# A transformer layer on one core: token norm, input projection and channel work made one stage that goes by blocks of 512 tokens

## Chip, cores and metric

The kernel runs on one core of a Trainium2 chip. The metric is the device time of one execution in microseconds, as the median of several. A profiled execution gives the rows below.

## What is computed

One layer of a diffusion backbone: 2048 latent tokens and a prefix of 256 context tokens, width 1024. The part that matters here is the way into the token mixer (in short form):

```python
h  = rmsnorm(x) * gain * (1 + scale) + shift      # scale, shift: c @ w_mod, other values for the context
z  = h @ w_in                                     # all columns of both branches and of the merge gates
p  = z[..., columns of the state branch]          # k, v, decay, rate; of latent tokens r and gate too
p  = p + mu[0] * (prev - p) + mu[1] * (nxt - p)   # neighbours in the sequence, zeros past its ends
kk = (k * k_k) / norm_of_head(k * k_k)            # then k * k_a, r * r_k, tanh(decay), sigmoid(gate) @ g2
```

After that come two branches (retention and a state recurrence by chunks), a merge, an output projection, and 16 experts. They are the same in both kernels.

## The kernel before

The program is a list of stages (`STAGES`, L2956). Each opens a room (buffers and semaphores) and gives every engine its own instruction stream; engines meet through semaphores alone, and a room ends when all have finished. SP issues loads and stores, POOL issues some transfers too, ACT (ScalarE) and DVE (VectorE) do elementwise work, PE (TensorE) the products. The first two stages, and the stage behind them, are in question:

- `projection` first makes the modulation vectors in a room `mod` from half of `w_mod` (8 loads of 1 MB). In `norm_rows` (L2161) the 18 token tiles of 128 tokens are loaded, squared and summed (ACT, L2212), scaled and turned by PE through a diagonal matrix (L2249), modulated (ACT and DVE), and split into a high and a low part, `hT`, kept for all 2304 tokens (L2300, L2302). The other 16 loads of `w_mod` and their products (L2157) lie in the same room. In `project` (L2307) a loop goes over the 46 column tiles of 128 columns; each tile's weights are loaded once (512 KB), split into high and low by ACT (L2360) and DVE (L2381), and multiplied with every block of tokens: 5 blocks (256 + 4 x 512) for tiles 0 to 17, which the context needs as well, and 4 for the rest. A product of one column tile with one block is 24 matmuls (8 slices of the inner dimension, each high*high, high*low and low*high, L106 to L108). ACT takes the result out (L2369) and SP writes whole rows of `zT` to DRAM.
- `rwkv_channels` (L207) reads 14 of those rows back, one row of 128 channels by 2305 positions at a time, and does the shift (L293, L295), the key norms (a contraction with ones on PE, a root on ACT, L300 and a product on DVE) and the gate's contraction (L361); POOL issues the stores (L379).
- `rwkv_chunks` follows and begins with SP's load of `ident` at L487.

What sets the order is the code of each engine, as written: an engine never passes an instruction that waits.

Of the kernel before, what the change touches and what calls it, by code (L numbers as in the profile page):

```python
# [112 lines left out]
def projection(nc, T):  # L113
# [3 lines left out]
    LATE = 4 * D // 256  # L117
    with Room(nc, "prj") as room:
# [6 lines left out]
        cond = room.sb("cond", [P, KT, 32])  # L125

        with Room(nc, "mod") as r0:
            small = r0.sb("small", [P, P])
            w = [r0.sb(f"w{g}", [P, KT, 256]) for g in range(EARLY)]
# [5 lines left out]
            w_in = [r0.sem(f"w_in{g}") for g in range(EARLY)]  # L135
# [3 lines left out]
            @block.sync  # L139
            def _(sp):  # L140
                sp.dma_start(ident[:, :], T["ident"]).then_inc(const_in, 16)
                sp.dma_start(pick[:, :], T["pick2"]).then_inc(const_in, 16)
                sp.wait_ge(zeroed, 1 + START)
                sp.dma_start(small[0:8, :], T["c"].rearrange("a (t p) -> (a t) p", p=P)).then_inc(rows_in, 16)
                sp.dma_start(small[8:16, :], T["c_ctx"].rearrange("(t p) -> t p", p=P)).then_inc(rows_in, 16)
                sp.dma_start(small[32:40, :], T["norm_g"][0, 0:1, :].rearrange("a (t p) -> (a t) p", p=P)).then_inc(rows_in, 16)
                sp.dma_start(small[64:112, :], T["b_mod"].rearrange("a (t p) -> (a t) p", p=P)).then_inc(rows_in, 16)
                for g in range(EARLY):
                    sp.dma_start(w[g][:, :, :], T["w_mod"][g]).then_inc(w_in[g], 16)
# [7 lines left out]
            def _(pe):  # L157
# [10 lines left out]
                for g in range(EARLY):  # L168
                    pe.wait_ge(w_in[g], 16 + START)
                    if g >= 4:  # L170
                        pe.wait_ge(moved, g - 3 + START)
                    contract(pe, acc[g % 4], cond, w[g]).then_inc(made, 1)
# [28 lines left out]
        with Room(nc, "prh") as rh:  # L201
            hT = [rh.sb("hT_hi", [P, KT, TOK], F32R), rh.sb("hT_lo", [P, KT, TOK], F32R)]
            norm_rows(nc, T, ident, pick, rowmod, scale, biasT, cond, hT)
            project(nc, T, hT)


def rwkv_channels(nc, T):  # L207


    W = TOK + 1  # L210
    SEGS = [(0, CTX, 0), (CTX + 1, W, CTX)]
    with Room(nc, "rch", start=0) as room:
        sb, sem = room.sb, room.sem
        ones = sb("ones", [P, P])
        g2 = sb("g2", [P, HALF])
        mu = sb("mu", [P, 14, 2])
        keep = sb("keep", [P, 14])
        par = sb("par", [P, 3, 4])
        tiny = sb("tiny", [P, 1])
        X = [sb(f"X{u}", [P, W + 2]) for u in range(3)]  # L220
        Y = [sb(f"Y{u}", [P, W]) for u in range(2)]
        norm = sb("norm", [P, W])
        ks = sb("ks", [P, W])
        kkn = sb("kkn", [P, W])
        kka = sb("kka", [P, W])
        rrk = sb("rrk", [P, W])
        gate = [sb(f"gate{u}", [P, TOK]) for u in range(2)]
        acc = room.ps("acc", [P, 5, 512])
        const_in, zeroed, keep_ok = sem("const_in"), sem("zeroed"), sem("keep_ok")
        x_in = [sem(f"x_in{u}") for u in range(3)]  # L230
        scaled, half, shifted = sem("scaled"), sem("half"), sem("shifted")
        squared, summed, rooted, ks_ok, kka_ok, recip, kkn_ok = [sem(n) for n in (
            "squared", "summed", "rooted", "ks_ok", "kka_ok", "recip", "kkn_ok")]
        rrk_ok, tanh_ok, sig_ok, g_made, g_ok = [sem(n) for n in ("rrk_ok", "tanh_ok", "sig_ok", "g_made", "g_ok")]
        y_out = [sem(f"y_out{u}") for u in range(2)]
        kkn_out, kka_out, rrk_out = sem("kkn_out"), sem("kka_out"), sem("rrk_out")
        g_out = [sem(f"g_out{u}") for u in range(2)]
        BL = [(512 * b, min(512, W - 512 * b)) for b in range(5)]
        zT = T["zT"].rearrange("(n p) t -> n p t", p=P)
        tiled = {n: T[n].rearrange("(n p) t -> n p t", p=P) for n in ("kS", "kkn", "kka", "vS", "rS", "rrk", "gT")}  # L240

        JOBS = [("wa", 0, Z_WA, 8), ("gd", 0, Z_GD, 13)]
        for p in range(4):
            JOBS += [("k", p, Z_K + p, p), ("r", p, Z_R + p, 9 + p), ("v", p, Z_V + p, 4 + p)]
        xbuf = [2 if kind == "r" else None for kind, *_ in JOBS]
        for n, j in enumerate(j for j, x in enumerate(xbuf) if x is None):
            xbuf[j] = n % 2

        def earlier(j, same):

            return max((i for i in range(j) if same[i] == same[j]), default=None)

        def loaded(j):

            return sum(16 if JOBS[i][0] == "r" else 32 for i in range(j + 1) if xbuf[i] == xbuf[j])

        def y_stored(j):

            return sum({"gd": 0}.get(JOBS[i][0], 32) for i in range(j % 2, j + 1, 2))
        block = room.block()  # L260

        @block.sync
        def _(sp):
            sp.dma_start(ones[:, :], T["head_ones"]).then_inc(const_in, 16)
            sp.dma_start(g2[:, :], T["rwkv_g2"][0]).then_inc(const_in, 16)
            with nc.allow_non_contiguous_dma("channel parameters over partitions"):
                for r in range(2):
                    sp.dma_start(mu[:, :, r], T["rwkv_mu"][0, r:r + 1, :].rearrange("a (t p) -> p (a t)", p=P)).then_inc(const_in, 16)
                for j, n in enumerate(("rwkv_k_k", "rwkv_k_a", "rwkv_r_k")):
                    sp.dma_start(par[:, j, :], T[n].rearrange("a (t p) -> p (a t)", p=P)).then_inc(const_in, 16)  # L270
            sp.wait_ge(zeroed, 3)
            for j, (kind, p, row, _) in enumerate(JOBS):
                before = earlier(j, xbuf)
                if before is not None:
                    sp.wait_ge(shifted, before + 1)
                x = X[xbuf[j]]
                for lo, hi, d in SEGS[kind == "r":]:
                    sp.dma_start(x[:, 1 + lo:1 + hi], zT[row, :, d:d + hi - lo]).then_inc(x_in[xbuf[j]], 16)

        @block.vector  # L280
        def _(ve):
            for x in X:
                ve.memset(x[:, :], 0.0).then_inc(zeroed, 1)
            ve.memset(tiny[:, :], 1e-12).then_inc(zeroed, 1)
            ve.wait_ge(const_in, 16 * 7)
            ve.tensor_tensor(keep[:, :], mu[:, :, 0], mu[:, :, 1], ALU.add).then_inc(zeroed, 1)
            ve.wait_ge(zeroed, 5)
            ve.tensor_scalar(keep[:, :], keep[:, :], -1.0, 1.0, ALU.mult, ALU.add).then_inc(keep_ok, 1)
            nk = 0
            for j, (kind, p, row, m) in enumerate(JOBS):  # L290
                x, y = X[xbuf[j]], Y[j % 2]
                ve.wait_ge(scaled, j + 1)
                ve.scalar_tensor_tensor(y[:, :], x[:, 0:W], mu[:, m, 0:1], y[:, :], ALU.mult, ALU.add).then_inc(half, 1)  # L293
                ve.wait_ge(half, j + 1)
                ve.scalar_tensor_tensor(y[:, :], x[:, 2:2 + W], mu[:, m, 1:2], y[:, :], ALU.mult, ALU.add).then_inc(shifted, 1)  # L295
                if j and JOBS[j - 1][0] == "k":

                    nk += 1
                    ve.wait_ge(rooted, nk)
                    ve.reciprocal(norm[:, :], norm[:, :]).then_inc(recip, 1)  # L300
                    ve.wait_ge(recip, nk)
                    ve.wait_ge(ks_ok, nk)
                    if nk > 1:
                        ve.wait_ge(kkn_out, 32 * (nk - 1))
                    ve.scalar_tensor_tensor(kkn[:, :], ks[:, :], -1.0, norm[:, :], ALU.mult, ALU.mult).then_inc(kkn_ok, 1)

        @block.scalar
        def _(act):
            act.wait_ge(const_in, 16 * 7)
            act.wait_ge(keep_ok, 1)  # L310
            nk = nr = 0
            for j, (kind, p, row, m) in enumerate(JOBS):
                x, y = X[xbuf[j]], Y[j % 2]
                act.wait_ge(x_in[xbuf[j]], loaded(j))
                if j >= 2:
                    act.wait_ge(y_out[j % 2], y_stored(j - 2))
                    if JOBS[j - 2][0] == "gd":
                        act.wait_ge(g_made, 16)
                act.activation(y[:, :], x[:, 1:1 + W], ACT.Copy, scale=keep[:, m:m + 1]).then_inc(scaled, 1)
                if j and JOBS[j - 1][0] == "k":  # L320

                    act.wait_ge(summed, nk)
# [1838 lines left out]
def norm_rows(nc, T, ident, pick, rowmod, scale, biasT, cond, hT):  # L2161
# [4 lines left out]
    with Room(nc, "nrm") as r1:  # L2166
# [39 lines left out]
        def _(act):  # L2206
# [11 lines left out]
            for n in range(NT):  # L2218
                u, r = n % 2, int(n < CT)
                if n + 1 < NT:  # L2220
                    sums_of(n + 1)
# [759 lines left out]
```

## Time and profile before

| | |
|---|---|
| median of three runs | 4955.49 us (4953.42 to 4962.13) |
| profiled execution, time | 4957.77 us |
| its span in the profile | 4956.0 us |
| TensorE busy | 4224.6 us (85%) |
| VectorE / ScalarE / GpSimd busy | 2297.6 / 1958.7 / 503.1 us |
| mean granted TensorE clock | 0.929 |
| moved by DMA | 637.78 MB, mean 129 GB/s |

The 1.8 us between time and span lie outside the profile. The three stages named above take the first 1438.43 us of the span.

### The profile page before, as it was taken

To read this page: it belongs to the slowest core of one execution; us is meant where nothing else is said; L and a number is where in the kernel's file an instruction comes from. 1 tells how busy PE (TensorE), PEld (TensorE's weight loads), DVE (VectorE), ACT (ScalarE), POOL (GpSimd) and SP (SyncE) were. 2 spreads that over 40 slices of the span, in tenths; PEclk is the share of its full clock that TensorE was granted. 3 is DMA by queue.
4 is the path that set the end of the run, shared out by engine and by line. 5 is a ranking of instruction groups with operands and counts; after the bars stand their busy time and mean duration, and the time that the engine had idled before them with its cause. 6 is when DMAs were issued, how large, how long until landed. Compare 5 with 4: busy or idle time off the path is not lost. (4 is left out here: it accounts for less than half of the span.)

```text
span 4956.0 us, 77358 instructions
## 1 busy us (share of the span) xinstructions
PE 4224.6 (85%) x29616; PEld 3561.7 (72%) x29616; DVE 2297.6 (46%) x3350; ACT 1958.7 (40%) x2956; POOL 503.1 (10%) x463
## 2 busy tenths in 40 slices
PE   6899999996229999999999968598946999999992
PEld 5788888885018888888888857476835888888882
DVE  4000000001656666666666658543564444444444
ACT  5111111112425655556555623511313444444443
POOL 0000000000121111111111103321001000000000
PEclk8999999998659999999999989599968999999996
DMA  7111121223641111211112133765416666666667
GB/s 281 68 69 69 68 76 64 76 76 106 244 159 47 46 46 50 58 46 46 46 48 59 46 111 103 195 228 184 161 50 246 214 220 208 207 216 216 216 207 271
DMA packets 348335, 637.78 MB, mean 129 GB/s; under 512 B 41772, under 2 KB 271636, under 8 KB 317896
## 3 DMA queue, kind: packets, MB, share of 16 engines
q1 hardware_dynamic: 328744, 542.95, 32.5%
q0 software_dynamic: 19488, 93.46, 5.8%
q8 instruction: 63, 1.03, 0.1%
q14 instruction: 40, 0.33, 0.0%
HBM read 474.92 MB, written 161.42 MB: 128 GB/s over the span
## 5 line engine op out<-in xcount | busy, mean ns | idle before, releaser
L106 PE MATMUL zp__acc<-prh__hT_hi,zp__wh 128*128 128x512 f32 (+1 forms) x1616 | 614.7, 380 | 9.4 <-DVE zp__wl L2381 9.4
L107 PE MATMUL zp__acc<-prh__hT_hi,zp__wl 128*128 128x512 f32 (+1 forms) x1616 | 614.6, 380 | 0.0
L108 PE MATMUL zp__acc<-prh__hT_lo,zp__wh 128*128 128x512 f32 (+1 forms) x1616 | 614.3, 380 | 0.0
L2040 DVE TENSOR_TENSOR exp__wl<-exp__raw,exp__wh 128x4096 fp32r<-128x4096 f32 x97 | 429.1, 4424 | 330.7 <-ACT exp__wh L1992 330.7
L2381 DVE TENSOR_TENSOR zp__wl<-zp__w,zp__wh 128x1024 fp32r<-128x1024 f32 x48 | 58.9, 1226 | 1009.5 <-ACT zp__wh L2360 1009.5
L1992 ACT ACTIVATE exp__wh<-exp__raw 128x4096 fp32r<-128x4096 f32 x97 | 352.2, 3631 | 291.3 <-PE exp__acc L108 191.6
L2369 ACT ACTIVATE zp__zo<-zp__acc 128x512 f32<-128x512 f32 (+1 forms) x202 | 117.0, 579 | 883.8 <-PE zp__acc L108 883.8
L106 PE MATMUL exp__acc<-exp__wh,exp__xh 128*128 128x512 f32 x1024 | 401.5, 392 | 2.5 <-DVE exp__xl L2045 2.5
L107 PE MATMUL exp__acc<-exp__wh,exp__xl 128*128 128x512 f32 x1024 | 399.2, 390 | 0.0
L108 PE MATMUL exp__acc<-exp__wl,exp__xh 128*128 128x512 f32 x1024 | 399.1, 390 | 0.0
L106 PEld LDWEIGHTS zp__acc<-prh__hT_hi,zp__wh 128*128 128x128 f32 x1616 | 305.1, 189 | 67.1 <-DVE zp__wl L2381 9.7
L107 PEld LDWEIGHTS zp__acc<-prh__hT_hi,zp__wl 128*128 128x128 f32 x1616 | 305.1, 189 | 57.4
L108 PEld LDWEIGHTS zp__acc<-prh__hT_lo,zp__wh 128*128 128x128 f32 x1616 | 305.0, 189 | 57.5
L599 ACT ACTIVATE rwc__Tb<-rwc__TP 128x512 bf16<-128x512 f32 x432 | 234.6, 597 | 279.5 <-PE rwc__TP L950 279.5
L799 DVE TENSOR_TENSOR rwc__Xb<-rwc__XB,rwc__level 128x512 bf16<-128x512 f32 x432 | 277.1, 683 | 110.5 <-PE rwc__XB L941 110.5
L106 PEld LDWEIGHTS exp__acc<-exp__wh,exp__xh 128*128 128x128 f32 x1024 | 192.7, 188 | 44.2 <-issue 2.9
L108 PEld LDWEIGHTS exp__acc<-exp__wl,exp__xh 128*128 128x128 f32 x1024 | 192.7, 188 | 40.4
L107 PEld LDWEIGHTS exp__acc<-exp__wh,exp__xl 128*128 128x128 f32 x1024 | 192.7, 188 | 39.3
L106 PE MATMUL exp__acc<-exp__wh,exp__hh 128*128 128x512 f32 x512 | 203.9, 398 | 0.0
L108 PE MATMUL exp__acc<-exp__wl,exp__hh 128*128 128x512 f32 x512 | 200.1, 391 | 0.0
L107 PE MATMUL exp__acc<-exp__wh,exp__hl 128*128 128x512 f32 x512 | 199.2, 389 | 0.0
L808 DVE TENSOR_TENSOR rwc__Gr<-rwc__PB,rwc__TT 128x512 f32<-128x512 f32 x222 | 153.2, 690 | 96.8 <-PE rwc__PB L985 91.0
(422 smaller groups left out, 8263.5 us busy)
## 6 DMA issues: line engine op xcount, KB each, us to landing
exp__raw<-in_w_x SPq DMA_DIRECT2D x98, 2048.0 KB, 7.8
s_zT<-zp__zo SPq DMA_DIRECT2D x28, 1024.0 KB, 4.5
zp__w<-in_w_z SPq DMA_DIRECT2D x48, 512.0 KB, 5.3
s_zT<-zp__zo SPq DMA_DIRECT2D x18, 1152.0 KB, 5.0
nrm__w<-in_w_mod POOLq DMA_DIRECT2D x16, 1024.0 KB, 7.7
brp__gate<-s_zT SPq DMA_DIRECT2D x32, 512.0 KB, 4.7
rch__X<-s_zT SPq DMA_DIRECT2D x14, 1024.0 KB, 6.6
rwc__kS<-s_kS SPq DMA_DIRECT2D x39, 256.0 KB, 3.0
```

What stands on the lines that cost most here:

```text
L106: pe.matmul(out, sh, mh, start=first, stop=False)
L107: pe.matmul(out, sl, mh, start=False, stop=False)
L108: return pe.matmul(out, sh, ml, start=False, stop=last)
L599: cp = lambda out, in_, n: act.activation(out, in_, ACT.Copy).then_inc(S[n], 1)
L799: tt(Xb[:, g, :, :], f4(XB[g]), level[:, d, l, None, :].to_broadcast([P, GH, C]), ALU.mult).then_inc(S["xd"], 1)
L808: tt(Gr[:, g, :, :], f4(PB[1]), TT32[:, g, :, :], ALU.add).then_inc(S["gd"], 1)
L1992: act.activation(wh[s][:, :, :], raw[s][:, :, :], ACT.Copy).then_inc(w_hi, 1)
L2040: ve.tensor_tensor(wl[s][:, :, :], raw[s][:, :, :], wh[s][:, :, :], ALU.subtract).then_inc(w_lo, 1)
L2369: act.activation(zo[u][:, lo:lo + n], acc[b][:, 0:n], fn).then_inc(kept, 1)
L2381: ve.tensor_tensor(wl[u][:, :, :], w[u][:, :, :], wh[u][:, :, :], ALU.subtract).then_inc(split_lo, 1)
```

## The change

`norm_rows`, the old `project` and `rwkv_channels` are replaced by one `project` in a room `fro`, which is written out in full (no loop on the engines) as 201 steps: block 0 (the context, 256 tokens) with the 17 column tiles that it needs, then each block of 512 latent tokens with all 46. At step s PE multiplies tile s, ACT takes out tile s-1 and splits the weights of s+2, DVE splits the same low, and SP loads the weights of s+3 into one of three buffers. So a column tile's weights are loaded and split once for each block, 201 times and not 48. `hT` is held for two blocks; the four token tiles of the next block are normalized at the first steps of the present one. Of the 46 tiles the 14 of the state branch come at every third step; ACT copies their results twice into a buffer in SBUF (`XY`), DVE shifts them there with two columns carried over from the block before (`halo`), and keys, queries and gates are finished a few steps later and stored by POOL's queue; their rows no longer go through `zT`. The 16 late products with `w_mod` lie in blocks 1 and 2. The first tokens, weights and channel parameters are loaded in the room `mod`, behind `w_mod`.

```diff
+                for u in range(3):
+                    sp.dma_start(xin[u][:, :], T["tokens"][u * P:(u + 1) * P, :]).then_inc(x_in[u], 16)
+                for u, (row, *_) in enumerate(CTX_TILES[0:3]):
+                    sp.dma_start(w[u][:, :, :], T["w_z"][row]).then_inc(w_in[u], 16)
...
-            norm_rows(nc, T, ident, pick, rowmod, scale, biasT, cond, hT)
-            project(nc, T, hT)
...
+        project(nc, T, ident, pick, rowmod, scale, biasT, cond, (w, w_in), (xin, x_in), (ones, g2, mu, par, chan_in))
...
+    ORDER = [(0,) + t for t in CTX_TILES] + [(b,) + t for b in range(1, 5) for t in LAT_TILES]
...
+            norm_at[base[b] + 4 * j] = 2 + 4 * b + j
...
+            for s in range(S + DRAIN):
+                if s + 3 < S:
+                    sp.wait_ge(split_lo, s + 1)
+                    sp.dma_start(w[s % 3][:, :, :], T["w_z"][ORDER[s + 3][1]]).then_inc(w_in[s % 3], 16)
...
+                if s - 3 in plain:
...
+                    sp.dma_start(zT[row, :, lo:lo + n], zo[plain[t] % 4][:, 0:n]).then_inc(z_out[plain[t] % 4], 16)
...
+            def split_high(s):
+                act.wait_ge(w_in[s % 3], 16 * (s // 3 + 1))
+                if s >= 3:
+                    act.wait_ge(made, s - 2)
+                act.activation(wh[s % 3][:, :, :], w[s % 3][:, :, :], ACT.Copy).then_inc(split_hi, 1)
...
+                act.activation(XY[i % 4][:, 0, 2:2 + n], acc[t % 3][:, 0:n], ACT.Copy)
+                act.activation(XY[i % 4][:, 1, 2:2 + n], acc[t % 3][:, 0:n], ACT.Copy, scale=keep[:, m:m + 1]).then_inc(kept, 1)
...
+                    act.activation(norm[c % 2][:, 0:n], y, ACT.Square, scale=par[:, 0, p:p + 1]).then_inc(squared, 1)
+                    act.activation(kka[c % 2][:, 0:n], y, ACT.Copy, scale=par[:, 1, p:p + 1]).then_inc(kka_ok, 1)
...
+            sums_of(1)
+            apply(0)
+            split_high(0)
+            apply(1)
+            split_high(1)
+            for s in range(S + DRAIN):
+                if 0 <= s - 1 < S:
+                    evict(s - 1)
+                if s + 2 < S:
+                    split_high(s + 2)
+                if s - 5 in keys_of:
+                    roots(s - 5)
...
+                if s - 3 in moved_of:
+                    follow(s - 3)
+                if s in norm_at:
+                    sums_of(norm_at[s])
+                if s - 3 in norm_at:
+                    apply(norm_at[s - 3])
...
+            turn(0)
+            turn(1)
+            for s in range(S + DRAIN):
+                if s < S:
+                    b = ORDER[s][0]
+                    n = BLOCKS[b][1]
+                    hi, lo = hT[b % 2]
+                    pe.wait_ge(split_lo, s + 1)
+                    if s == base[b]:
+                        pe.wait_ge(lo_done, CT + 4 * b)
+                    if s >= 3:
+                        pe.wait_ge(kept, s - 2)
+                    for k in range(KT):
+                        mm = product(pe, acc[s % 3][:, 0:n], (wh[s % 3][:, k, :], wl[s % 3][:, k, :]), (hi[:, k, 0:n], lo[:, k, 0:n]),
+                                     k == 0, k == KT - 1)
+                    mm.then_inc(made, 1)
+                t = s - 4
+                if t in keys_of:
...
+                    contracted(ones[:, :], norm[keys_of[t] % 2], end - j0)
...
+                if s - 2 in norm_at:
+                    turn(norm_at[s - 2])
...
+                    contract(pe, macc, cond, wm[g % 2]).then_inc(mod_made, 1)
...
+                ve.tensor_copy(hi, hv[:, :, :]).then_inc(hi_done, 1)
...
+                ve.tensor_tensor(lo, hv[:, :, :], hi, ALU.subtract).then_inc(lo_done, 1)
...
+            def split_low(s):
+                ve.wait_ge(split_hi, s + 1)
+                if s >= 3:
+                    ve.wait_ge(made, s - 2)
+                ve.tensor_tensor(wl[s % 3][:, :, :], w[s % 3][:, :, :], wh[s % 3][:, :, :], ALU.subtract).then_inc(split_lo, 1)
...
+            def shift(t):
...
+                ve.tensor_copy(xy[:, :, 0:2], halo[:, m, :, :]).then_inc(halo_in, 1)
...
+                ve.scalar_tensor_tensor(y, xy[:, 0, j0:end], mu[:, m, 0:1], y, ALU.mult, ALU.add).then_inc(half, 1)
...
+                ve.scalar_tensor_tensor(y, xy[:, 0, j0 + 2:end + 2], mu[:, m, 1:2], y, ALU.mult, ALU.add).then_inc(shifted, 1)
...
+            ve.wait_ge(chan_in, 16 * 7)
...
+            inverse(0)
+            inverse(1)
+            apply(0)
+            split_rows(0)
+            split_low(0)
+            apply(1)
+            split_rows(1)
+            split_low(1)
+            for s in range(S + DRAIN):
+                if s + 2 < S:
+                    split_low(s + 2)
+                if s - 2 in moved_of:
+                    shift(s - 2)
+                if s - 6 in keys_of:
+                    keys(s - 6)
+                if s - 1 in norm_at:
+                    inverse(norm_at[s - 1])
+                if s - 3 in norm_at:
+                    apply(norm_at[s - 3])
+                if s - 4 in norm_at:
+                    split_rows(norm_at[s - 4])
...
+    ctx = [(Z_K + p, "k", p, ACT.Copy) for p in range(4)] + [(Z_WA, "wa", 0, ACT.Copy)] + [(Z_V + p, "v", p, ACT.Copy) for p in range(4)]
+    plain = [(Z_RK + p, "z", 0, ACT.Copy) for p in range(8)]
+    first = [ctx[i // 2] if i % 2 == 0 else plain[i // 2] for i in range(17)]
+    turned = ctx[0:4] + [ctx[5], ctx[4], (Z_GD, "gd", 0, ACT.Copy)] + ctx[6:9] + [(Z_R + p, "r", p, ACT.Copy) for p in range(4)]
+    plain = (plain + [(Z_RQ + p, "z", 0, ACT.Copy) for p in range(4)] + [(Z_RG + p, "z", 0, ACT.Silu) for p in range(4)]
+             + [(Z_MG + p, "z", 0, ACT.Sigmoid) for p in range(16)])
+    rest, nt, np_ = [], 0, 0
+    for i in range(46):
+        if i % 3 == 1 and nt < 14:
+            rest.append(turned[nt])
+            nt += 1
+        else:
+            rest.append(plain[np_])
+            np_ += 1
+    return first, rest
...
-STAGES = (projection, rwkv_channels, rwkv_chunks, retention, rwkv_output,
+STAGES = (projection, rwkv_chunks, retention, rwkv_output,
           branch_products, mixer_output, choose, experts, output)
```

On PE, in the norm room of the kernel before (`tp` is the turned token tile, `acc` a product with `w_mod`, `mT` its turned rows), a whole room of such rows stands ahead of the first projection product:

```order
L2249 MATMUL nrm__tp<-nrm__dg,nrm__xin 128x128 x24
L2157 MATMUL nrm__acc<-nrm__w,prj__cond 32x256 x8
L2249 MATMUL nrm__tp<-nrm__dg,nrm__xin 128x128 x8
L2157 MATMUL nrm__acc<-nrm__w,prj__cond 32x256 x8
L2255 MATMUL nrm__mT<-prj__pick,nrm__ev 128x2 x2
```

In the changed kernel PE has these rows at steps of block 1 (`acc` is a projection tile, `rc` the key sums, `tp` a token tile of block 2):

```order
L106 MATMUL fro__acc<-fro__hT_hi,fro__wh 128x512
L107 MATMUL fro__acc<-fro__hT_hi,fro__wl 128x512
L108 MATMUL fro__acc<-fro__hT_lo,fro__wh 128x512
L2269 MATMUL fro__rc<-fro__norm,prj__ones 128x511
L2264 MATMUL fro__tp<-fro__dg,prj__xin 128x128 x8
```

The turns and the key sums have moved in between two tiles of the projection.

On DVE, at the same place of the program before, the norm ends and a loop with nothing but weight splits (`wl`) begins:

```order
L2296 TENSOR_SCALAR nrm__hv<-nrm__tp,prj__scale,prj__rowmod 128x128 x2
L2300 CAST prh__hT_hi<-nrm__hv 128x8x128
L2302 TENSOR_TENSOR prh__hT_lo<-nrm__hv,prh__hT_hi 128x8x128
L2304 TENSOR_TENSOR nrm__late<-nrm__mT,prj__biasT 128x32
L61 UNCONDITIONAL_BRANCH
L2376 UNCONDITIONAL_BRANCH
L2378 UNCONDITIONAL_BRANCH
L2378 ISA
L2381 TENSOR_TENSOR zp__wl<-zp__w,zp__wh 128x1024
```

In the changed kernel DVE has these rows in block 1, from one weight split to the fourth after it (L2367 to L2377 are a shift, L2384 and L2388 the keys, L2340 to L2352 a token tile of block 2):

```order
L2358 TENSOR_TENSOR fro__wl<-prj__w,fro__wh 128x1024
L2367 COPY fro__XY<-fro__halo 128x2x2
L2372 COPY fro__halo<-fro__XY 128x4
L2375 SCALAR_TENSOR_TENSOR fro__XY<-fro__XY,prj__mu 128x511
L2377 SCALAR_TENSOR_TENSOR fro__XY<-fro__XY,prj__mu 128x511
L2358 TENSOR_TENSOR fro__wl<-prj__w,fro__wh 128x1024
L2384 RECIPROCAL fro__norm<-fro__norm 128x511
L2388 SCALAR_TENSOR_TENSOR fro__kkn<-fro__XY,fro__nkk,fro__norm 128x511
L2340 TENSOR_SCALAR fro__hv<-fro__tp,prj__scale,prj__rowmod 128x128 x4
L2358 TENSOR_TENSOR fro__wl<-prj__w,fro__wh 128x1024
L2350 CAST fro__hT_hi<-fro__hv 128x8x128
L2352 TENSOR_TENSOR fro__hT_lo<-fro__hv,fro__hT_hi 128x8x128
```

Shift, keys and norm have moved in between the weight splits, of which each now serves one block.

## Rows read from the trace of the kernel before

**Rows 1.** Windows: stretch, us, busy and count per engine, granted clock, DMA share, GB/s
```profile
35.78:137.78 102.00, 66.80 (x610) 53.21 (x610) 54.28 (x112) 71.83 (x182) 8.77 (x16) 0.85 0.74 269
137.78:1193.50 1055.72, 1055.69 (x4848) 882.99 (x4848) 56.36 (x46) 171.81 (x256) 0.00 (x0) 1.00 0.20 70
1193.50:1438.43 244.93, 42.29 (x72) 17.78 (x72) 148.61 (x43) 89.36 (x55) 28.90 (x54) 0.59 0.58 209
```

**Rows 2.** Timeline, first instructions of norm_rows on SP and ACT
```profile
35.78 10.94 SPq L2193 DMA_DIRECT2D nrm__xin<-in_tokens  x4
...
39.26 1.06 ACT L2212 ACTIVATE nrm__sq<-nrm__xin 128x1024 bf16<-128x1024 f32 x1 [32.85 <-DMA nrm__xin<-in_tokens]
...
46.40 0.81 ACT L2235 ACTIVATE nrm__hv<-nrm__tp,prj__rowmod,prj__scale 128x128 f32<-128x128 f32 x2 [3.02 <-PE nrm__tp L2249]
```

**Rows 3.** Timeline, POOL and SP: start, us, instruction, idle before and its releaser
```profile
1422.85 1.07 POOL L379 DMA_DIRECT2D s_vS<-rch__Y  x2 [4.12 <-DVE rch__Y L295]
...
1438.43 0.33 SPq L487 DMA_DIRECT2D rwc__ident<-in_ident  x1
```

**Rows 4.** Timeline, ACT in the stream: evictions of the projection
```profile
143.20 0.39 ACT L2369 ACTIVATE zp__zo<-zp__acc 128x256 f32<-128x256 f32 x1 [5.50 <-PE zp__acc L108]
...
165.01 0.60 ACT L2369 ACTIVATE zp__zo<-zp__acc 128x512 f32<-128x512 f32 x1 [4.84 <-PE zp__acc L108]
167.88 0.38 ACT L2369 ACTIVATE zp__zo<-zp__acc 128x256 f32<-128x256 f32 x1 [1.33 <-PE zp__acc L108]
```

**Rows 5.** Timeline, DVE in branch_products: gatings of two tiles in a row
```profile
3301.83 0.69 DVE L1370 TENSOR_TENSOR brp__t<-brp__acc,brp__gate 128x512 f32<-128x512 f32 x1 [2.13 <-PE brp__acc L108]
...
3307.27 0.69 DVE L1370 TENSOR_TENSOR brp__t<-brp__acc,brp__gate 128x512 f32<-128x512 f32 x1 [2.13 <-PE brp__acc L108]
```

**Rows 6.** Timeline, PE at the end of norm_rows
```profile
98.03 2.05 PE L2249 MATMUL nrm__tp<-nrm__dg,nrm__xin 128*128 128x128 f32 x16 [0.23 <-DVE nrm__dg L2286]
100.25 1.07 PE L2157 MATMUL nrm__acc<-nrm__w,prj__cond 128*32 128x256 f32 x16 [0.17 <-DMA nrm__w<-in_w_mod]
101.25 0.61 PE L2255 MATMUL nrm__mT<-prj__pick,nrm__ev 128*128 128x2 f32 x4
```

**Rows 7.** Lines: group, count, busy us, mean ns, idle before and releaser
```profile
L2381 DVE TENSOR_TENSOR zp__wl<-zp__w,zp__wh 128x1024 fp32r<-128x1024 f32 x48 | 58.9, 1226 | 1009.5 <-ACT zp__wh L2360 1009.5
L2360 ACT ACTIVATE zp__wh<-zp__w 128x1024 fp32r<-128x1024 f32 x48 | 50.5, 1051 | 6.9 <-DMA zp__w<-in_w_z 6.9
L2369 ACT ACT_TABLE_LOAD x10 | 12.8, 1283 | 0.2
L2302 DVE TENSOR_TENSOR prh__hT_lo<-nrm__hv,prh__hT_hi 128x1024 fp32r<-128x1024 f32 x18 | 22.1, 1226 | 0.6
L2300 DVE CAST prh__hT_hi<-nrm__hv 128x1024 fp32r<-128x1024 f32 x4 | 2.8, 694 | 6.4 <-ACT nrm__hv L2235 6.4
L2296 DVE TENSOR_SCALAR nrm__hv<-nrm__tp,prj__scale,prj__rowmod 128x128 f32<-128x128 f32 x6 | 2.2, 403 | 0.0
L300 DVE RECIPROCAL rch__norm<-rch__norm 128x2305 f32<-128x2305 f32 x4 | 58.2, 14558 | 0.0
L293 DVE SCALAR_TENSOR_TENSOR rch__Y<-rch__X,rch__mu,rch__Y 128x2305 f32<-128x2305 f32 x14 | 36.7, 2620 | 73.9 <-ACT rch__Y L319 73.9
```

**Rows 8.** DMA by time from 0 to 60 us: 40 slices of 1.5 us
```profile
GB/s 0 0 47 66 257 421 426 431 421 421 421 431 431 431 421 421 410 208 11 0 0 0 0 0 109 404 385 404 442 401 284 85 281 259 101 0 0 319 156 393
```

**Rows 9.** DMA from 1199 to 1207 us: the channel parameters' packets
```profile
q1 hardware_dynamic: 5488, 0.35, 52.1%
```

**Rows 10.** Timeline, PE in rwkv_channels: the gate's contractions
```profile
1231.39 15.86 PE L361 MATMUL rch__acc<-rch__Y,rch__g 128*128 128x512 f32 x32 [37.93 <-ACT rch__Y L341]
```

**Rows 11.** DMA issues: queue, count, KB each, median us to landing
```profile
zp__w<-in_w_z SPq DMA_DIRECT2D x48, 512.0 KB, 5.3
mod__w<-in_w_mod SPq DMA_DIRECT2D x8, 1024.0 KB, 11.8
```

More of the change, by code:

```diff
@@ L116, in projection @@
     EARLY = 2 * D // 256
-    LATE = 4 * D // 256
     with Room(nc, "prj") as room:
@@ L2158, in contract, with project @@
     return m
[L2161 to L2164 removed]
+def project(nc, T, ident, pick, rowmod, scale, biasT, cond, weights, tokens, channels):
+    (w, w_in), (xin, x_in), (ones, g2, mu, par, chan_in) = weights, tokens, channels
     EARLY, LATE = 2 * D // 256, 4 * D // 256
[L2166 to L2184 removed]
@@ new lines, in project, with count @@
+    BLOCKS = [(0, CTX)] + [(CTX + 512 * b, 512) for b in range(4)]
+    ORDER = [(0,) + t for t in CTX_TILES] + [(b,) + t for b in range(1, 5) for t in LAT_TILES]
+    S = len(ORDER)
+    base = [0] + [len(CTX_TILES) + len(LAT_TILES) * (b - 1) for b in range(1, 5)]
+    MU = {"k": 0, "v": 4, "wa": 8, "r": 9, "gd": 13}
+    def count(kinds):
+        n, out = 0, {}
+        for s, (b, row, kind, p, fn) in enumerate(ORDER):
+            if kind in kinds:
+                out[s] = n
+                n += 1
+        return out
@@ new lines, in project, with y_stores, span @@
+    plain, moved_of = count(("z",)), count(tuple(MU))
+    keys_of, quer_of, gate_of, wa_of = count(("k",)), count(("r",)), count(("gd",)), count(("wa",))
+    stored_of = {s: (0 if ORDER[s][2] == "gd" else 1) for s in moved_of}
+    def y_stores(i):
+        return sum(stored_of[s] for s, n in moved_of.items() if n % 4 == i % 4 and n < i)
+    before4 = {n: s for s, n in moved_of.items()}
+    def span(s):
+        b = ORDER[s][0]
+        lo, n = BLOCKS[b]
+        j0, end = int(b in (0, 1)), n + int(b in (0, 4))
+        return j0, end, lo - 1 + j0
@@ L2198, in _ @@
         @block.gpsimd
         def _(gp):
-            for g in range(LATE):
-                if g >= 2:
-                    gp.wait_ge(made, g - 1 + START)
-                gp.dma_start(w[g % 2][:, :, :], T["w_mod"][EARLY + g]).then_inc(w_in[g % 2], 16)
+            gp.memset(zero[:, :], 0.0).then_inc(zeroed, 1)
+            gp.memset(halo[:, :, :, :], 0.0).then_inc(zeroed, 1)
+            gp.wait_ge(zeroed, 2)
+            for name in ("rS", "rrk"):
+                for q in range(4):
+                    gp.dma_start(tiled[name][q, :, 0:CTX], zero[:, :]).then_inc(zero_out, 16)
@@ L2237, in _, with apply @@
-            act.wait_ge(late_t, 1 + START)
-            act.activation(lateT[:, :], mt[0:4 * KT, 0:P], ACT.Copy).then_inc(late_r, 1)
+            def apply(n):
+                r = int(n < CT)
+                act.wait_ge(turned, n + 1)
+                if n:
+                    act.wait_ge(lo_done, n)
+                for k in range(4):
+                    ins = act.activation(hv[:, k, :], tp[0][:, k, :], ACT.Identity, scale=scale[:, k, r:r + 1], bias=rowmod[:, 0, k, r:r + 1])
+                ins.then_inc(hv_a, 1)
@@ new lines, in roots, with gates @@
+            def roots(t):
+                c = keys_of[t]
+                j0, end, at = span(t)
+                act.wait_ge(summed, use_of[t, 0] + 1)
+                act.activation(norm[c % 2][:, 0:end - j0], rcf[:, 0:end - j0], ACT.Sqrt, bias=tiny[:, :]).then_inc(read, 1)
+            def gates(t, q):
+                i = 4 * gate_of[t] + q
+                j0, end, at = span(t)
+                act.wait_ge(summed, use_of[t, q] + 1)
+                if i >= 2:
+                    act.wait_ge(g_out[q % 2], 16 * (i // 2))
+                act.activation(gate[q % 2][:, 0:end - j0], rcf[:, 0:end - j0], ACT.Copy).then_inc(read, 1)
@@ L2250, in turn @@
                 t.then_inc(turned, 1)
-            def rows(g):
-                pe.wait_ge(moved, g + 1 + START)
-                for h in range(2):
-                    m = pe.matmul(mT[:, 4 * g + 2 * h:4 * g + 2 * h + 2], ev[g % 2][:, h * P:(h + 1) * P], pick[:, :], start=True, stop=True)
-                m.then_inc(added, 1)
-            def weights(g):
-                pe.wait_ge(w_in[g % 2], 16 * (g // 2 + 1))
-                if g >= 2:
-                    pe.wait_ge(moved, g - 1 + START)
-                contract(pe, acc[g % 2], cond, w[g % 2]).then_inc(made, 1)
@@ L2263, in _, with contracted @@
-            for n in range(NT):
-                turn(n)
-                if n >= 2:
-                    weights(n - 2)
-                if n >= 3:
-                    rows(n - 3)
-            rows(LATE - 1)
-            pe.wait_ge(late_ok, 1 + START)
-            pe.transpose(mt[0:4 * KT, 0:P], late[:, :], ident[:, :]).then_inc(late_t, 1)
+            def contracted(stat, mov, n):
+                m = min(n, 512)
+                mm = pe.matmul(rc[:, 0, 0:m], stat, mov[:, 0:m], start=True, stop=True)
+                if n > 512:
+                    mm = pe.matmul(rc[:, 1, 0:n - 512], stat, mov[:, 512:n], start=True, stop=True)
+                mm.then_inc(summed, 1)
@@ new lines, in apply, with split_rows @@
+            def apply(n):
+                r = int(n < CT)
+                ve.wait_ge(turned, n + 1)
+                if n:
+                    ve.wait_ge(lo_done, n)
+                for k in range(4, KT):
+                    ins = ve.tensor_scalar(hv[:, k, :], tp[1][:, k - 4, :], scale[:, k, r:r + 1], rowmod[:, 0, k, r:r + 1], ALU.mult, ALU.add)
+                ins.then_inc(hv_v, 1)
+            def split_rows(n):
+                b, c = (0, n) if n < CT else (1 + (n - CT) // 4, (n - CT) % 4)
+                hi, lo = [t[:, :, c * P:(c + 1) * P] for t in hT[b % 2]]
+                ve.wait_ge(hv_a, n + 1)
+                ve.wait_ge(hv_v, n + 1)
+                if b >= 2 and c == 0:
+                    ve.wait_ge(made, base[b - 1])
+                ve.tensor_copy(hi, hv[:, :, :]).then_inc(hi_done, 1)
+                ve.wait_ge(hi_done, n + 1)
+                ve.tensor_tensor(lo, hv[:, :, :], hi, ALU.subtract).then_inc(lo_done, 1)
@@ new lines, in keys @@
+            def keys(t):
+                c, i, p = keys_of[t], moved_of[t], ORDER[t][3]
+                j0, end, at = span(t)
+                n = end - j0
+                ve.wait_ge(read, use_of[t, 0] + 1)
+                ve.reciprocal(norm[c % 2][:, 0:n], norm[c % 2][:, 0:n]).then_inc(recip, 1)
+                ve.wait_ge(recip, c + 1)
+                if c >= 2:
+                    ve.wait_ge(kkn_out[c % 2], 16 * (c // 2))
+                ve.scalar_tensor_tensor(kkn[c % 2][:, 0:n], XY[i % 4][:, 1, 1 + j0:1 + end], nkk[:, p:p + 1], norm[c % 2][:, 0:n],
+                                        ALU.mult, ALU.mult).then_inc(kkn_ok, 1)
@@ new lines, in _ @@
+            ve.wait_ge(keep_ok, 3)
+            inverse(0)
[6 more added lines that the diff above has]
+            split_low(1)
+            for s in range(S + DRAIN):
+                if s + 2 < S:
[10 more added lines that the diff above has]
+                    split_rows(norm_at[s - 4])
+                if s == last_rows + 2:
+                    ve.wait_ge(mod_added, LATE)
+                    ve.tensor_tensor(late[:, :], mT.rearrange("p (t r) -> p t r", r=2)[:, :, 0], biasT[:, 2 * KT:6 * KT], ALU.add).then_inc(late_ok, 1)
```

598 lines of the change are left out of this document (245 added, 353 removed).

## The prediction

> **What bounds the kernel now.** The chain of waits covers only the end of the program here, so I cut the span into windows at the borders of the stages and looked in each for the engine that never rests [rows 1]. From 137.78 to 1193.50 us, the stream of projection products, TensorE is busy 1055.69 of 1055.72 us at a granted clock of 1.00. The other engines are nearly idle: VectorE 56, ScalarE 172 us, DMA at 0.20. Ahead of it the norm stretch of 102.00 us has TensorE busy for 66.8 us, but with turns and `w_mod` products, none of them a projection product. Behind it lies the channel stretch of 244.93 us, with TensorE at 42.29 us. These two cannot overlap the stream, since the rooms follow each other. So the sum to be attacked is 102.00 + 1055.72 + 244.93 = 1402.65 us, and only 1056 of it is bound by products. The rest of the program has the same code, and I let it stay.
>
> The borders: SP's first token load stands at 35.78 us [rows 2], and the first load of the stage behind at 1438.43 us [rows 3]. I work out the time between the same two points after the change.
>
> **The products that remain.** An eviction ends each tile. The 512-token tile before the eviction at 165.01 and the 256-token tile that ends at 167.88 us stand 2.87 us apart [rows 4], so 24 matmuls on 256 tokens take 2.87 us. The very first such tile ran from 137.78 to 143.20 us, 5.4 us, nearly twice as long: behind a pause TensorE runs at the lower of its two clock levels, and the granted clock of the stretch ahead is 0.85 [rows 1]. The stream holds 18 context tiles and 184 others, which gives (1055.72 - 5.4 - 17 x 2.87) / 184 = 5.443 us for one of 512 tokens. The changed kernel has the same 184, and 17 instead of 18 for the context. Its code is written out and not looped; a stage that is written out already, `branch_products`, has two gatings of 24 matmuls each from 3301.83 to 3307.27 us, 5.44 us [rows 5]. So I charge nothing for the form of the code.
>
> Blocks 1 to 4: 184 x 5.443 = **1001 us**.
>
> **Block 0.** TensorE needs 17 x 2.87 = 48.8 us at full clock, four turns for block 1 (2.05 us each [rows 6]) and four key sums of about 0.5 us (half of a contraction of 512 columns, below): 59 us. VectorE has as much: 17 weight splits of 1.226 us, four token tiles of about 4 us (four modulations of 0.40, a cast of 0.69, a split of 1.23), nine shifts of about 1 us and four key tails of about 2 us, which I scale down from 14.56 and 2.62 us for 2305 columns [rows 7]; in all 54 us. ScalarE comes to about 48 us. Three engines with the same load and fixed orders cannot all be hidden behind one another, and their pauses may cost TensorE its clock: 17 tiles at 5.4 us would be 92 us. I take the middle of 59 and 92, rounded down, **74 us**, and keep both ends.
>
> **The start.** The last loads of `w_mod` land by about 26 us, where the traffic falls from 410 to 11 GB/s [rows 8]. Behind them the new loads bring 3.1 MB of tokens and weights; at the 421 GB/s of the slices before, that is 7.4 us. The channel parameters are small packets: as they were loaded before, they took 52% of 8 us on all 16 engines, 4.2 us [rows 9]. So all has landed at about 38 us, when ScalarE has squared the first tokens; VectorE, which waits for the parameters first, is held up by little, by at most 3.5 us if they land as late as 41.5. From the first square to the first modulation the trace has 46.40 - 39.26 = 7.1 us [rows 2]; then two token tiles on VectorE (3.5 us each) and one weight split of 1.2 us. With the first square at 36 us the first product comes at 52 to 55 us: **17 us** behind the border, 3 more or less. In the norm stretch it was 102.
>
> **What moves onto TensorE in blocks 1 to 4.** Twelve turns of 2.05 us, 16 products with `w_mod` of 1.07 + 0.61 us [rows 6], and 16 key sums and 16 gate contractions. The gate's 32 matmul records are 16 contractions in 15.86 us, 0.99 each [rows 10]. Turns, `w_mod` and the 32 contractions: 24.6 + 26.9 + 31.7 = **83 us**, all on the path, because TensorE is the bound there. Before, they lay in the stretches that go.
>
> **What is hidden.** The 153 added weight splits cost ScalarE 153 x 1.051 = 161 us and VectorE 153 x 1.226 = 188 us [rows 7]. I add them to the work of the three windows [rows 1]: ScalarE 333 + 161, with some 14 us of table loads more (11 of 1.28 us), makes 508 us; VectorE 259 + 188 makes 447 us. That is 43% and 38% of a stage of 1190 us. The splits are made for two tiles ahead, and the longest stretch of other work between two splits on VectorE (keys and four modulations) is about 5.5 us, half of the 10.9 us that two tiles leave. If that cover failed at every piece, the price is in rival A. Weights: a load is issued when the buffer's last split is done, and the next round of three tiles takes 16.3 us, of which the two splits and their starts need 2.6; a landing of up to 13.7 us costs nothing. The loads took 5.3 us, and 11.8 when eight of twice the size were queued together [rows 11].
>
> The Trainium skill (DMA: Bandwidth & Descriptors, Specifications) puts the limit of a core's HBM traffic at about 358 GB/s. That speaks against reading weights four times more. This trace has slices of 421 to 431 GB/s [rows 8], so the row decides. By the Trainium skill's figure, the 3.1 MB at the start would be an estimated 8.7 us instead of 7.4, and the sum 1.3 us longer; the stage's traffic stays below either.
>
> **The tail.** After the last product comes its eviction (0.60 us [rows 4]), a store, and the end of the room. Before, the last store of the channel stage ended at 1423.92 us and the next stage's load stood at 1438.43, 14.5 us later [rows 3]. With 0.4 us for the issue: **15.5 us**.
>
> **The sum.** 17 + 74 + 1001 + 83 + 15.5 = 1190.5 us, against 1402.65: 212 us less. From the profiled time of 4957.77 us that makes 4745.6; that execution was 2.3 us above the median, so on the median's scale it is 4955.49 - 212 = **4743 us**.
>
> **Rivals.**
> *A: ScalarE and VectorE do not keep up piece by piece.* Orders are fixed, so a weight split stands behind shifts, roots, keys and norm pieces, and TensorE waits where several fall together. For it: in block 0 the loads are equal, and each of the 21 table loads holds ScalarE up for 1.28 us. Against it: two tiles of slack, and loads below 45%. Full price in blocks 1 to 4: 16 key tails of 3.9 us and 12 token tiles of 4 us open on TensorE, 110 us; half of it is 55. That gives 4798 to 4853 us.
> *B, on the other side: weights land too late.* All transfers share the queues' engines: weights at 512 KB for each 5.44 us, 96 GB/s, with stores of `zT`, channel stores and `w_mod` beside them. For it: the same data are read four times more often. Against it: 5.3 us as measured, and a total of some 198 MB in 1190 us, 166 GB/s (201 loads are 105 MB; tokens, `w_mod` and the stores, counted from their shapes, the rest), where 421 were seen. Above a landing of 13.7 us each further 3 us cost 1 us per tile; the gain of 212 us is used up at 1.15 us on each of 184 tiles, a landing of 17.2 us. At 20 us the time would be 4955 + 184 x 2.1 - 212 = 5129 us.
> *C: the written-out code is fetched late, or TensorE stays at half clock in block 0.* [rows 5] speak against the first; block 0 at 92 us gives 4761, inside the range.
>
> **Chances.** The forecast with its own range of 4720 to 4790 (block 0 from 59 to 92, start and tail together 8 either way, some 20 us of exposed pieces) has 0.73. Rival A from 4790 up to 4853 has 0.13. Rival B has 0.06, half of that slower than before and half a gain that is only smaller. C beyond block 0, and anything between A and no change, 0.03. Faster than 4720 (the room ends sooner, VectorE's loads in block 0 fit) has 0.05. The range from 4720 to 4812 leaves out 0.05 below, and above it the upper part of A, B and the rest, about 0.14. A difference below 0.2%, about 10 us, could not be told from no change in this kernel: faster by more than that 0.95, within it 0.01, slower 0.04.
>
> **What would show it.** In the profile after: the first projection product at 52 to 55 us; evictions in blocks 1 to 4 at 5.44 us, with pauses of 2.05 us for a turn, about 1 us for sums and 1.7 us for `w_mod`; TensorE busy throughout at clock 1.00 with no wait for `fro__wl`; the stage's end near 1226 us; weights landing in 5 to 8 us. It is wrong if TensorE's idle in blocks 1 to 4 is over 30 us and ends on VectorE's weight split (A) or if ScalarE's split there waits for DMA (B), if the tile pitch itself is not 5.44, or if the stages behind change by more than 5 us.

## The result, and the profile after

The changed kernel takes 4818.12 us (median of 4, 4816.60 to 4819.19), the kernel before in the same job 4958.81 us: a ratio of 0.9717, interval 0.9700 to 0.9734. That is 141 us faster, where 212 were forecast, and above the range of 4720 to 4812 us.

Windows of the changed kernel, columns as in [rows 1]: the start, block 0, blocks 1 to 4, the tail of the stage, and the stage behind it (`rwkv_chunks`, the recurrence), up to the first load of the next:

```profile
35.78:56.91 21.13, 7.54 (x33) 7.01 (x33) 9.26 (x23) 10.14 (x19) 4.93 (x10) 1.00 0.31 76
56.91:123.48 66.57, 61.89 (x485) 60.56 (x486) 53.38 (x91) 45.37 (x89) 9.69 (x18) 0.96 0.76 248
123.48:1204.55 1081.07, 1080.44 (x5006) 876.34 (x5004) 425.81 (x538) 425.80 (x626) 70.98 (x131) 1.00 0.53 166
1204.55:1213.32 8.77, 0.00 (x0) 0.00 (x0) 0.00 (x0) 0.00 (x1) 0.00 (x1) 0.65 0.08 30
1213.32:2765.41 1552.09, 1338.97 (x14520) 1190.38 (x14556) 977.48 (x1686) 852.80 (x1569) 243.26 (x207) 0.96 0.18 51
```

The first four windows are the stage that was forecast: 1177.5 us against 1402.65 of before. It gains 225 us, 13 more than forecast, and in blocks 1 to 4 TensorE is busy for 1080.44 of 1081.07 us. The loss is in the fifth, in code that the change does not touch. The same window of the kernel before:

```profile
1438.43:2913.17 1474.74, 1316.52 (x14556) 1170.67 (x14556) 976.15 (x1686) 850.69 (x1570) 243.34 (x207) 0.98 0.19 52
```

The same code, busy times within 2% on every engine, and 77.3 us more. The waits of TensorE in that window (us, times, longest) have one entry that the kernel before does not have at all, and the timeline shows where it falls:

```profile
PE rwc__TP L741 <- issue: 67.1, 28, 4.5
```

```profile
1335.04 0.61 PE L741 MATMUL rwc__TP<-rwc__identb,rwc__TTb 128*128 128x128 bf16 x4 [4.19 <-issue]
...
1418.20 0.60 PE L741 MATMUL rwc__TP<-rwc__identb,rwc__TTb 128*128 128x128 bf16 x4 [4.07 <-issue]
```

L741 is the first product of the loop's body. The loop has 18 rounds (288 records of that line, 16 a round), and at each of the 17 returns to its head, 83.16 us apart here and 77.6 in the kernel before, TensorE stands for 3 to 4.5 us and waits for no engine and no data. Such a wait also costs clock (the last columns are granted clock, DMA share and GB/s). The 4 us from the first of the two rows above, and the same 4 us in the run with 196 instructions (below), where this round's first product stands at 1335.16 us without a wait:

```profile
1335.00:1339.00 4.00, 3.49 (x22) 2.76 (x24) 1.43 (x3) 1.19 (x2) 0.00 (x0) 0.50 0.18 41
```

```profile
1335.00:1339.00 4.00, 3.06 (x32) 2.36 (x31) 2.23 (x5) 2.48 (x5) 0.00 (x0) 1.00 1.01 272
```

So the 77.3 us are 67.1 us of waits at L741 and 22.5 us by which TensorE is busy longer, less some 12 us of other waits that are gone. The queue that carries instructions tells what it waits for. Its row on the page of before, and then of after:

```profile
q8 instruction: 63, 1.03, 0.1%
```

```profile
q8 instruction: 246, 4.03, 0.4%
```

And in the window of the recurrence alone, before and after:

```profile
q8 instruction: 9, 0.15, 0.0%
```

```profile
q8 instruction: 162, 2.65, 0.7%
```

The packets have 16 KB each, and 162 = 9 + 17 x 9: the 9 of before, and nine more for each return. At each return the loop is fetched anew.

### The profile page after: what moved, and what is told of

Read it like the earlier page. It is cut to its first block and busy times, and to the rows that moved or that the text cites. A ratio compares the mean times of both kernels' runs of the same rounds, so it can differ in the third digit from the quotient of the medians.

```text
span 4815.7 us, 78091 instructions
## 1 busy us (share of the span) xinstructions
PE 4239.0 (88%) x29572; PEld 3575.6 (74%) x29608; DVE 2528.8 (53%) x3801; ACT 2108.8 (44%) x3195; POOL 550.6 (11%) x552
## 5 line engine op out<-in xcount | busy, mean ns | idle before, releaser
L106 PE MATMUL fro__acc<-fro__hT_hi,fro__wh 128*128 128x512 f32 (+1 forms) x1608 | 625.3, 389 | 6.6 <-DVE fro__hT_lo L2352 3.7
L107 PE MATMUL fro__acc<-fro__hT_hi,fro__wl 128*128 128x512 f32 (+1 forms) x1608 | 613.0, 381 | 0.0
L108 PE MATMUL fro__acc<-fro__hT_lo,fro__wh 128*128 128x512 f32 (+1 forms) x1608 | 612.8, 381 | 0.0
L2358 DVE TENSOR_TENSOR fro__wl<-prj__w,fro__wh 128x1024 fp32r<-128x1024 f32 x201 | 246.2, 1225 | 644.9 <-ACT fro__wh L2162 644.9
L106 PEld LDWEIGHTS fro__acc<-fro__hT_hi,fro__wh 128*128 128x128 f32 x1608 | 303.6, 189 | 73.0 <-issue 17.3
L107 PEld LDWEIGHTS fro__acc<-fro__hT_hi,fro__wl 128*128 128x128 f32 x1608 | 303.7, 189 | 59.2 <-issue 3.6
L108 PEld LDWEIGHTS fro__acc<-fro__hT_lo,fro__wh 128*128 128x128 f32 x1608 | 303.4, 189 | 58.6
L2172 ACT ACTIVATE fro__zo<-fro__acc 128x512 f32<-128x512 f32 (+1 forms) x136 | 79.6, 585 | 477.2 <-PE fro__acc L108 473.6
L2162 ACT ACTIVATE fro__wh<-prj__w 128x1024 fp32r<-128x1024 f32 x201 | 211.8, 1054 | 0.0
```

The costliest lines, as they stand in the source:

```text
L106: pe.matmul(out, sh, mh, start=first, stop=False)
L107: pe.matmul(out, sl, mh, start=False, stop=False)
L108: return pe.matmul(out, sh, ml, start=False, stop=last)
L2162: act.activation(wh[s % 3][:, :, :], w[s % 3][:, :, :], ACT.Copy).then_inc(split_hi, 1)
L2172: act.activation(zo[i % 4][:, 0:n], acc[t % 3][:, 0:n], fn).then_inc(kept, 1)
L2358: ve.tensor_tensor(wl[s % 3][:, :, :], w[s % 3][:, :, :], wh[s % 3][:, :, :], ALU.subtract).then_inc(split_lo, 1)
```

## Experiments

Theory F: the loop has 1704 instructions on TensorE (all counts of instructions are from the compiled programs), and where it begins decides whether it stays on the chip. Rivals: its data lie or arrive otherwise (D), or the clock (C, which is not the prediction's rival C). The edit, in `rwkv_chunks`, of the changed kernel or of the kernel before, with N = 392 or 80 (two waits make one instruction):

```diff
+            for _ in range(N):
+                pe.wait_ge(const_in, START)
             pe.wait_ge(const_in, 16 * 14 + START)
```

**196 instructions in the changed kernel.** 

> The changed kernel with 392 waits that are already satisfied (196 instructions in the compiled program) on TensorE at the head of the recurrence stage, where TensorE waits for its first data anyway; nothing else differs. Theory F (code loading): the stage's loop has 1704 instructions on TensorE and its place in the program decides whether it stays on the chip; instruction 12053 instead of 11857 moves the loop 21 instead of 81 behind a multiple of 256. The stage falls back to about 1467 us, the one wait of 4.2 us in each round goes, and the time is 4818 - 75 = 4743 us, between 4735 and 4755. Theory D (the recurrence is slower because its data are written and read in another way): nothing changes, 4810 to 4830. Theory C (the clock): nothing changes.

**40 in the changed kernel.** 

> The same with 80 waits (40 instructions), so the loop stands 121 behind a multiple of 256. Theory F: still the bad place, 4818 us, between 4810 and 4828, and the wait of 4.2 us in each round stays. If any shift or the added waits themselves were what helps, it would fall as with 196.

**40 in the kernel before.** 

> The kernel before with the 40 instructions at the same place; its loop moves from 63 to 103 behind a multiple of 256. Theory F: it loses what the changed kernel lost, 4957 + 75 = 5032 us, between 5020 and 5040, with a wait of about 4.2 us in each round of the recurrence. Theories D and C: 4950 to 4965, since no data and no stage changes.

**196 in the kernel before.** 

> The kernel before with 196 instructions, loop at 3 behind a multiple of 256. Theory F: a good place as before, 4957 us, between 4948 and 4968. If the added waits cost by themselves, it would be some 10 us longer.

Measured, in this order: 4741.96 (ratio 0.9556, 0.9540 to 0.9572), 4829.22 (1 us above its range), 5028.09 (5003.58 and 5052.60; ratio 1.0131, 1.0073 to 1.0189) and 4963.00 us, against 4961.39 of before. Waits alone win the whole loss back, and in another number make the kernel before lose. The recurrence with 196 instructions has the busy times of before and is 3.8 us longer; its window, and the instruction queue's row on its page:

```profile
1213.06:2691.64 1478.58, 1316.69 (x14556) 1170.70 (x14556) 975.99 (x1686) 849.38 (x1569) 242.97 (x207) 0.98 0.18 52
```

```profile
q8 instruction: 94, 1.54, 0.1%
```

The kernel before with 40 instructions has the new wait in 7 rounds of the profiled execution, the one of 5003.58 us (a row of its waits):

```profile
PE rwc__TP L934 <- issue: 37.4, 7, 6.2
```

Its instruction queue has 126 packets, 63 = 7 x 9 more than before. Why some rounds are spared there stays open. D and C fall as causes: no data moved, and with the wait gone the granted clock is 0.98 again, so the lower clock follows from the waits.

**Which places are bad.** The same edit, further along.

> The changed kernel with 296 instructions (592 satisfied waits) at the same place, 256 more than in the run with 40: the loop stands at 12153, again 121 behind a multiple of 256. If only the place within 256 instructions counts (theory F, code is loaded in blocks of 256 instructions), the recurrence is slow again: 4829 us as with 40 instructions, 4810 to 4840. If it is the number of added instructions or the pause that they make that helped (theory P), the time stays at 4742 us as with 196.

> The same with 238 instructions: the loop at 12095, 63 behind a multiple of 256, where it stands in the kernel before. Theory F: fast, 4742 us, 4735 to 4752. If there were another cause in the data or stages ahead that the 196 instructions hid by accident, a slow time of 4818 us would come back.

> The run with 238 instructions was slow though its loop stands at the place of the kernel before, counted by 256; so the unit is not 256 instructions of the program, or not from its first. Two countings fit all seven places run so far (before, changed, and 196, 40, 296 and 238 instructions there, 40 and 196 in the kernel before): N, blocks that hold 255 instructions of the program, places 79, 68 and 20 fast and 110 and above slow; M, blocks of 256 with a few loop labels left out, places up to about 60 and from about 230 up fast, 63 to 121 slow. With 134 instructions the loop starts at 11991: by N place 6, fast, 4742 us (4735 to 4752); by M place 215, slow, 4810 to 4840 us.

> 220 instructions, the loop at 12077. By N place 92, between the fast 79 and the slow 110, and slow if the loop's 1704 instructions may reach over 7 blocks of 255 (which leaves 81): 4810 to 4840 us. By M place 45, fast: 4742 us (4735 to 4752).

| loop begins at | counted by M | median us | packets of q8 |
|---|---|---|---|
| 4159 (before) | 59 | 4958.81 | 63 |
| 4355 (before, 196) | 255 | 4963.00 | 64 |
| 12053 (196) | 21 | 4741.96 | 94 |
| 12077 (220) | 45 | 4743.87 | 94 |
| 12095 (238) | 63 | 4811.36 | 175 |
| 11857 (changed) | 81 | 4818.12 | 246 |
| 4199 (before, 40) | 99 | 5028.09 (of 5003.58 and 5052.60) | 126 (at 5003.58) |
| 11897 (40), 12153 (296) | 121 | 4829.22, 4841.90 | 246, 248 |
| 11991 (134) | 215 | 4871.94 | 247 |

The run with 296 instructions is slow, so neither their number nor their pause is what helps. The one with 238 was expected fast and came out slow: counted straight by 256, my places were wrong. Of the two countings that I then set against each other, N as it was stated fell in both runs and M held: the place modulo 256, with the four loop labels that stand ahead in the kernel before left out (4159 - 4 = 4155, place 59). Fast are 255, 21, 45 and 59, slow 63, 81, 99, 121 and 215; 4871.94 us at 215 lies 32 us above M's range, and why a round costs more there stays open. That the labels drop out is only argued from this fit. Nor is M the only counting that is left: by 255 the fast places are 20, 68, 79 and 92, the slow ones 110 to 168 and 6, so an N whose stretch of good places lies elsewhere fits all runs too, with no label left out. The traces lean to 256: in the written-out stage of the ten runs of the changed kernel and its variants TensorE has 255.7 to 255.9 records for each packet of its instruction queue (42 or 43 packets in each trace). That the place of the loop decides, and not the waits or their number, is shown; the exact count is not.

The Trainium skill (Runtime: NRT & Kernel Launch, Instruction fetch mechanics) gives TensorE 128 KiB for 2048 instructions, refilled in blocks of 16 KiB or 256 instructions, and says that a jump to a block outside the window that is held costs a fetch. The trace agrees on the block, 2.65 MB in 162 packets. The page counts two blocks for that window; in the kernel before the whole loop stays, with 9 packets in all 18 rounds, and the measurement decides. By the page's sizes 1704 instructions lie in seven or in eight of eight blocks, an estimate; the page does not say that eight are too many, and the runs show that from one place on the loop is lost. By the same estimate it is seven blocks from 89 of the 256 places; if M's count began 26 to 29 instructions earlier, every fast place would lie among these and every slow one outside. No run tests that.

**Each weight split made twice**, in the kernel with 196 instructions; the same on VectorE:

```diff
-                act.activation(wh[s % 3][:, :, :], w[s % 3][:, :, :], ACT.Copy).then_inc(split_hi, 1)
+                act.activation(wh[s % 3][:, :, :], w[s % 3][:, :, :], ACT.Copy).then_inc(once_hi, 1)
+                act.wait_ge(once_hi, s + 1)
+                act.activation(wh[s % 3][:, :, :], w[s % 3][:, :, :], ACT.Copy).then_inc(split_hi, 1)
```

> The kernel with the 196 instructions, and in it each of the 201 weight splits is made twice on ScalarE and on VectorE, the second after the first (402 instead of 201 on each: 211 and 246 us more). If the splits are hidden beside the products, as the prediction says, only block 0 grows, where VectorE would come to 75 us: 4742 + 5 to 20 us, 4747 to 4762 us. If the splits stand in the path piece by piece (rival A), at least a quarter of the 246 us comes out: 4800 us and more.

**Each weight load made twice:**

```diff
+                    sp.dma_start(spare[:, :, :], T["w_z"][ORDER[s + 3][1]]).then_inc(spare_in, 16)
```

> The kernel with the 196 instructions, and each of the last 198 weight loads of the stage is made a second time, into a spare buffer that nobody reads: 104 MB more in 1178 us. If a landing of up to 13.7 us costs nothing, as the prediction says, then the landing of the weights rises from 4.2 us to perhaps 6, and the time stays at 4742 us, 4735 to 4752. By rival B (the transfers are the bound) each tile would be held up: with a landing of 17 us, 4742 + 184 x 1.1 = 4944 us.

Measured: 4756.38 us for the splits, 4754.15 (4749.46 to 4758.84) for the loads. From the first eviction of block 1 to the last of block 4, windows of the kernel with 196 instructions, with splits twice, and with loads twice:

```profile
128.68:1203.70 1075.02, 1074.98 (x4985) 871.99 (x4983) 425.87 (x538) 425.18 (x626) 70.72 (x131) 1.00 0.53 165
```

```profile
149.21:1224.26 1075.05, 1075.01 (x4985) 871.92 (x4983) 646.16 (x719) 616.70 (x807) 70.72 (x131) 1.00 0.53 165
```

```profile
138.10:1213.13 1075.03, 1074.99 (x4985) 872.11 (x4983) 425.73 (x538) 425.19 (x626) 70.70 (x131) 1.00 0.78 254
```

VectorE with 220 us more, ScalarE with 192, DMA at 254 instead of 165 GB/s: the stretch stays at 1075.0 us. Splits and loads are hidden in blocks 1 to 4. What the stage lost, it lost ahead of the first eviction of block 1, at 128.68, 149.21 and 138.10 us. In block 0 a tile has 2.87 us, not 5.44, and the second splits are not free. For the loads I had not expected a loss (4754.15 us is 2 above the range), and it does not show that traffic costs time there: the landing rose only from 4.3 to 4.5 us, but the edit makes SP wait for each spare load before it issues the next, and in block 0 (55 to 140 us) that held SP up:

```profile
SPq L2065 <- DMA fro__spare<-in_w_z: 59.4, 17, 7.1
```

The next tile's weights are issued behind this wait, and ScalarE waited 16.9 us for weights there.

**Channel parameters loaded ahead of tokens and weights** (the block of seven loads moved up), in the kernel with 196 instructions:

> The kernel with the 196 instructions, and the channel parameters are loaded ahead of the first tokens and weights instead of behind them. If the first square waits for the parameters (through VectorE's keep factors), it comes 3 us earlier, at 36 us instead of 39.2, and with it the first product, at 53 to 54 instead of 56.9 us: the time falls by 3 us to about 4739 us, which only the trace can tell, not the times. If tokens or weights then land too late, the first product stays at 57 us or comes later.

Measured: 4734.06 us (4729.47 to 4734.90, 4 runs), a ratio of 0.9541 (0.9525 to 0.9557), the lowest median here; by the ratios it can't be told from the 0.9556 without this edit. The traces can: the first square stands at 35.60 instead of 40.58 us, the first product at 50.93 instead of 55.80, and the next stage's first load at 1208.41 instead of 1213.06. So it is some 5 us, where 3 were expected.

## Why the prediction was wrong

The step that failed is the sentence "The rest of the program has the same code, and I let it stay", together with "So I charge nothing for the form of the code". Inside the stage the written-out code does cost nothing: 225 us of gain with no wait of TensorE in blocks 1 to 4 to speak of. But it moves a loop that comes later from instruction 4159 to 11857, and that loop then is fetched anew at each return to its head, for 77 us. The rows that the prediction had on written-out code [rows 5] tell how it runs itself, and nothing of a loop behind it. With the loop at a good place the kernel takes 4741.96 us, 1 us from the forecast. That it is so near is luck: the terms of the stage were off by 4 to 7 us, in sum 13 us too long, and the kernel before took 4961.39 us in that job, so that the gain was 219 us and not 212. The prediction's own test, "if the stages behind change by more than 5 us", names the symptom, but no rival had the mechanism; rival C looked for late code only in the new stage.

| term | forecast | measured |
|---|---|---|
| start, to the first product | 17 | 21.1 |
| block 0 | 74 | 66.6 |
| blocks 1 to 4, 184 tiles of 5.44 | 1001 | 1001 |
| work moved onto TensorE | 83 | 79 |
| tail | 15.5 | 9.4 |
| sum | 1190.5 | 1177.5 |
| recurrence behind | 0 | +77 |
| all other stages | 0 | +7.5 |

Block 0 is from the first product to 5.44 us ahead of block 1's first eviction (128.92 us); the moved work is 1080.5 - 1001.5 from there to the last eviction at 1203.95.

- *Start.* It was the parameters, but on another path. I priced their packets (4.2 us) and let VectorE alone wait for them. SP's time to issue them was not in the sum: the whole room `mod` ends only when SP has issued its loads (the last issue ends at 38.26 us, the stage's first instruction stands at 39.18), and ScalarE's first square needs VectorE's keep factors. SP and ScalarE, in the changed kernel's timeline:

```profile
22.50 13.41 SPq L164 DMA_DIRECT2D prj__mu<-in_rwkv_mu  x2
...
40.65 1.06 ACT L2145 ACTIVATE fro__sq<-prj__xin 128x1024 bf16<-128x1024 f32 x1 [34.21 <-DVE fro__keep L2398]
```

- *Block 0.* The middle of 59 and 92 was 7 us too high. TensorE was granted 0.96, so half the clock for all of it was not near.
- *Rivals A and B* are refuted for blocks 1 to 4 by the two runs that doubled their cost. In block 0 A works on a small scale; for B no run shows it, since there the doubled loads held SP up by a wait of their own.
- *Tail.* The room's end took 8.8 us behind the last eviction, not the 14.5 behind a last store by POOL's queue; here SP's store of `zT` is the last.
- *The other stages'* 7.5 us: `mixer_output` has 3.1 of it, `branch_products` 1.6 (first to last instruction). With 196 instructions `mixer_output` still is 1.1 longer than before. Their cause was not looked for.

## What to carry to other kernels

A change that writes code out, or takes code away, moves every loop behind it. Compare a later stage's own span in both traces before believing in a gain; if it grew with equal busy times, look for waits on "issue" at the head of a loop's body and at the packets of the instruction queue. Satisfied waits ahead of the loop, where the engine pauses anyway, tell it, and repair it if their number brings the loop to a good place: here 196 and 220 instructions did, 40, 134, 238 and 296 did not. Work on engines that are 40% busy was hidden to the last microsecond where a tile has 5.44 us, and not where it has 2.87.

## What the hardware showed that was not expected

- A loop of 1704 instructions on TensorE is fetched again, in nine packets of 16 KB, at each return to its head from some places and not at all from others; a return costs 4.5 us at place 81 (77 / 17) and 7.6 at place 215 (130 / 17, against the 4741.96 us). At places 63 and 99 only 9 and 7 of the 17 returns of the profiled execution were hit, by the packets (81 and 63).
- Behind such a wait of 4 us the granted clock of TensorE was 0.50 for the next 4 us, the lower of its two levels; without it, 1.00.
- SP needs 13.41 us to issue two loads of 7 KB in small packets (`mu`) behind 3 MB of others; ahead of them, right behind `w_mod`, 18.60 us, but from 9.88 us on, so that it ends earlier. The row of the run with the parameters first:

```profile
9.88 18.60 SPq L160 DMA_DIRECT2D prj__mu<-in_rwkv_mu  x2
```
